# Forget-gate bias and causal mask of the last attention: from GpSimd tiles in SBUF to matmuls in PSUM and VectorE adds

## The reference

```
def odd_layer(x, norm_g, w_in, b_forget, w_out):
    hn = rmsnorm(x, norm_g)
    q, k, v, z, f_logit = jnp.split(hn @ w_in, cuts, axis=-1)      # 16 heads of 128
    log_f = jax.nn.log_sigmoid(f_logit + b_forget)                 # (tokens, 16)
    o = forgetting_attention(q, k, v, log_f)
    return x + (o * jax.nn.silu(z)) @ w_out

# logit[t,s] = q_t.k_s/sqrt(dh) + sum_{s<j<=t} log f_j, causal
    cum = cumsum(log_f)                                            # per head
    s = einsum(q, k) * scale + cq[..., None] - cum[:, :, None, :]
    s = where(kpos <= qpos, s, -inf);  p = softmax(s);  o = einsum(p, v)
```

## Time and profile before

| | |
|---|---|
| median of three executions | 3194.14 us (3189.12 to 3198.18) |
| profiled execution, device time | 3198.18 us |
| its span in the trace | 3196.4 us |
| TensorE busy / VectorE / ScalarE / GpSimd | 94% / 48% / 26% / 9% |
| mean granted TensorE clock | 0.973 of full |

### The profile page before, as it was taken

The page is one execution under the profiler, slowest core; times in us unless marked ns, Lnnn a source line. Parts: engine busy times, 40 slices in busy tenths (PEclk is TensorE's granted clock), DMA queues, the critical chain, the costliest instruction groups (busy, mean ns, idle before and its releaser), DMA issues.

```text
span 3196.4 us, 42548 instructions
## 1 busy us (share of the span) xinstructions
PE 3009.0 (94%) x18244; PEld 2161.4 (68%) x18244; DVE 1547.4 (48%) x1846; ACT 837.8 (26%) x926; POOL 283.5 (9%) x260
## 2 busy tenths in 40 slices
PE   8999999899999999999999999879999998999898
PEld 6777777899977743333333333268858878998886
DVE  4465544674556522222222222357887554444765
ACT  3352221544434310110110110010000243444443
POOL 2042111000000000000000000035440000000100
PEclk9999988999998999999999999989999999999999
DMA  7543221446575599999999999843333355898543
GB/s 244 151 139 100 74 61 58 123 140 182 174 237 171 190 366 425 425 425 425 425 425 425 425 425 425 341 159 118 114 124 118 126 178 125 194 194 183 137 165 138
DMA packets 216144, 725.25 MB, mean 227 GB/s; under 512 B 16314, under 2 KB 18794, under 8 KB 165644
## 3 DMA queue, kind: packets, MB, share of 16 engines
q1 hardware_dynamic: 210716, 702.22, 62.6%
q0 software_dynamic: 4144, 18.14, 1.6%
q10 hardware_dynamic: 1088, 2.10, 0.2%
HBM read 720.28 MB, written 2.11 MB: 226 GB/s over the span
## 4 chain that ended last, share of the span: by engine, by line
PE 72%; DMA 12%; DVE 11%; ACT 4%; issue 1%; POOL 0%; DVEq 0%; ACTq 0%
PE psum L137 71%; DMA t<-in_w_up 12%; DVE t L283 8%; ACT t L254 2%; PE psum L143 2%; DVE t L294 1%; ACT t L256 1%; DVE t L298 1%; DVE t L306 0%; ACT L254 0%; POOL t L328 0%; DVE t L269 0%; ACT L256 0%; DMA t<-in_x 0%; DVE t L275 0%
## 5 line engine op out<-in xcount | busy, mean ns | idle before, releaser
L137 PE MATMUL psum<-t,t 128*128 128x256 f32 (+7 forms) x17166 | 2914.8, 379 | 135.3 <-DVE t L283 78.8
L137 PEld LDWEIGHTS psum<-t,t 128*128 128x128 f32 (+4 forms) x17166 | 2069.7, 175 | 941.2 <-issue 564.2
L283 DVE TENSOR_TENSOR t<-t,t 128x1024 fp32r<-128x1024 f32 (+6 forms) x642 | 786.0, 1224 | 495.8 <-ACT t L254 462.5
L254 ACT ACTIVATE t<-t 128x1024 fp32r<-128x1024 f32 (+8 forms) x521 | 528.6, 1015 | 901.4 <-PE psum L137 625.3
L283 DVE TENSOR_TENSOR t<-t,psum 128x1024 f32<-128x1024 f32 (+3 forms) x265 | 246.3, 929 | 741.3 <-PE psum L137 440.7
L254 ACT ACTIVATE t<-psum 128x1024 f32<-128x1024 f32 (+5 forms) x278 | 213.5, 768 | 1414.9 <-PE psum L137 1315.5
L328 POOL TENSOR_TENSOR t<-t,t 128x1024 f32<-128x1024 f32 (+8 forms) x133 | 222.9, 1676 | 571.7 <-DVE t L283 258.2
L283 DVE TENSOR_TENSOR t<-psum,t 128x1024 f32<-128x1024 f32 (+6 forms) x117 | 101.1, 864 | 121.9 <-PE psum L137 91.8
L143 PE MATMUL psum<-t,t 128*128 128x128 f32 (+1 forms) x566 | 87.9, 294 | 31.7 <-DVE t L294 18.0
L143 PEld LDWEIGHTS psum<-t,t 128*128 128x128 f32 (+1 forms) x566 | 67.6, 150 | 69.5 <-issue 39.8
L83 POOL DMA_DIRECT2D t<-in_s_lr x1 | 0.6, 574 | 1187.2 <-DVE t L306 1187.2
(11 more groups left out here) (67 smaller groups left out, 240.1 us busy)
## 6 DMA issues: line engine op xcount, KB each, us to landing
t<-in_w_gate SPq DMA_DIRECT2D x128, 1024.0 KB, 16.9
t<-in_w_up SPq DMA_DIRECT2D x128, 1024.0 KB, 18.4
t<-in_w_down SPq DMA_DIRECT2D x128, 1024.0 KB, 17.5
t<-in_w_in SPq DMA_DIRECT2D x160, 512.0 KB, 4.1
t<-in_w_in_odd SPq DMA_DIRECT2D x128, 512.0 KB, 5.4
t<-in_w_in_even SPq DMA_DIRECT2D x96, 512.0 KB, 3.8
t<-in_w_out SPq DMA_DIRECT2D x32, 512.0 KB, 4.3
t<-in_w_pg SPq DMA_DIRECT2D x32, 512.0 KB, 4.3
```

Source lines behind the costliest of these rows:

```text
L137: ins = self.e.matmul(o, l, r, start=start, stop=stop, skip_group_check=True)
L254: self.put(self.e.activation(o, i, f, scale=scale), event)
L283: self.put(self.e.tensor_tensor(o, a, b, op), event)
```

## The change

The bias is no longer made as a tile. On TensorE, every score matmul is followed by one more into the same place, which adds F: its stationary operand is a selector `selo` of 16 partitions by 128 columns that holds ones in the row of head h, and its moving operand is F with 16 partitions and 128 or 256 columns. On DVE, each `masked` becomes three operations: an add of the mask on the first 128 columns of both heads, a copy of the middle 128, an add of the mask on the last 128. On GpSimd, the transfers and the eight additions are gone; instead it fills the selector once (a memset and an affine select of 128x2048), after the even layer has released that memory. The wait of `masked` on GpSimd goes; TensorE waits for F and for the selector ahead of scores.

```
-        forget = [alloc(1536).rearrange("p (h x) -> p h x", h=4) for _ in range(2)]
-        f_rows = nc.dram_tensor("f_rows", (16, 256), F32, kind="Internal").ap()
+        selo = alloc(16 * 128).rearrange("p (h t) -> p h t", h=16)
...
-                        pe.wait_ge(("od.q.c", 3), ("od.k.c", 3))
+                        pe.wait_ge(("od.q.c", 3), ("od.k.c", 3), ("od.F",), ("od.sel",))
...
-                            pe.mm(o[:, 0:128], qTo[:, h, 0:128], kTo[:, h, 0:128], True, True)
-                            pe.mm(o[:, 128:384], qTo[:, h, 128:256], kTo[:, h, :], True, True,
+                            pe.mm(o[:, 0:128], qTo[:, h, 0:128], kTo[:, h, 0:128], True, False)
+                            pe.mm(o[:, 0:128], selo[0:16, h, :], F[0][:, 0:128], False, True)
+                            pe.mm(o[:, 128:384], qTo[:, h, 128:256], kTo[:, h, :], True, False)
+                            pe.mm(o[:, 128:384], selo[0:16, h, :], F[0], False, True,
                                   event=("od.s", u, g2) if j else None)
...
-                    v.wait_ge(("od.s", u, g2), ("od.fm", u))
+                    v.wait_ge(("od.s", u, g2))
                     if u > 1:
                         v.wait_ge(("od.p", u - 2, 1))
-                    v.tt(s4[:, 2 * g2:2 * g2 + 2, :], po[:, :, 0:384], forget[u % 2][:, 2 * g2:2 * g2 + 2, :], ALU.add,
-                         event=("od.scored", u) if g2 else None)
+                    v.tt(so[:, :, 0:128], po[:, :, 0:128], cmb, ALU.add)
+                    v.copy(so[:, :, 128:256], po[:, :, 128:256])
+                    v.tt(so[:, :, 256:384], po[:, :, 256:384], cmb, ALU.add)
                     v.free("od.s", u, g2)
...
-            g.wait_ge(("ev.oT", 3), ("ev.oT", 5), ("od.F",))
-            g.load(("landed.rows",), [(f_rows, F[0])])
-            g.wait_ge(("landed.rows",))
-            for u in range(4):
...
-                g.tt(fm[:, :, 0:128], fm[:, :, 0:128], cmb, ALU.add)
-                g.tt(fm[:, :, 256:384], fm[:, :, 256:384], cmb, ALU.add, event=("od.fm", u))
+            g.wait_ge(("ev.oT", 3), ("ev.oT", 5))
+            selector(selo, ("od.sel",))
```

More of the change, by code:

```diff
@@ L2190, in masked @@
                     s4 = scso[u % 2].rearrange("p (h x) -> p h x", h=4)
+                    cmb = cmask.unsqueeze(1).broadcast_to([128, 2, 128])
                     po = v.bank("od.s", u, g2).rearrange("p (a x) -> p a x", a=2)
-                    v.wait_ge(("od.s", u, g2), ("od.fm", u))
+                    so = s4[:, 2 * g2:2 * g2 + 2, :]
+                    v.wait_ge(("od.s", u, g2))
                     if u > 1:
                         v.wait_ge(("od.p", u - 2, 1))
-                    v.tt(s4[:, 2 * g2:2 * g2 + 2, :], po[:, :, 0:384], forget[u % 2][:, 2 * g2:2 * g2 + 2, :], ALU.add,
-                         event=("od.scored", u) if g2 else None)
+                    v.tt(so[:, :, 0:128], po[:, :, 0:128], cmb, ALU.add)
+                    v.copy(so[:, :, 128:256], po[:, :, 128:256])
+                    v.tt(so[:, :, 256:384], po[:, :, 256:384], cmb, ALU.add)
                     v.free("od.s", u, g2)
```

## The result

The changed kernel takes 3217.1 us (median of four executions, 3214.1 to 3222.57) against 3194.2 before: a ratio of 1.0073, 95% interval 1.0054 to 1.009, so 23 us slower (17 to 29). Three more executions of it took 3210.2 to 3220.02 us. The prediction said 3199, between 3191 and 3208. The time lies outside the range, and about five times as far from the kernel before as the forecast.

The account below looks back on a forecast made before the run. TensorE and VectorE were taken to alternate as the bound, with VectorE last in turns 1 to 3. 2.62 + 3 x 0.70 = 4.7 us on the median of 3194.14 gave 3199 us; range 3191 to 3208.

Parts of the forecast that it names:

- So few rows save nothing, and a group gains 1.31 us: Score groups on TensorE: 16-row selector matmuls cost as much as 128-row ones; 2.62 us a turn, 10.5 us in four turns.
- The first rival: Turns 1 to 3: TensorE's price paid in full, 13.3 us if nothing is hidden, 3207.4 us; chance 0.15, including most of it.
- the margin of 0.2 us in turns 2 and 3: Before z13: TensorE would come 0.49 us later, VectorE 0.70 later, so VectorE is last by 0.2 us.
- the wait of 0.98 before z13: Turn 2: third TensorE wait for VectorE in the old timeline, after 0.37 and 1.76; not in the forecast's room.
- the 2.13: Turn 2: TensorE's waits in front of z13, 0.37 + 1.76 us, set against its added 2.62 us.
- half clock behind waits alone: Slow stretches after TensorE waits cost 1.0 to 1.5 us each; taken as zero in the sum, ends +1.5 and -1.5.
- turn 3's slow stretch: After 1.76 us of waiting, granted clock 0.50 over 3050.20 to 3053.60; said to be on the path, -1.5 if it vanishes.
- The sum: Turns 0 to 3: 2.62 us in turn 0 plus 0.70 in each of three turns, together 4.7 us slower.
- the half clock at z7: Turn 1: the wait before z7 grows from 2.78 to 4.6 us; +1.5 if its slow stretch gets longer.
- VectorE's term: Masked adds: three operations for one add cost 0.35 us more a group, 0.70 a turn, on the chain in turns 1 to 3.
- the 2.62 of scores(0): Turn 0: scores(0) stands on TensorE in front of z0, so its whole added 2.62 us is paid.
- GpSimd's side: Selector fill costs nothing, at most +1 us; removed additions return about 1 us of VectorE where TensorE had work: nothing.

Follow-up runs that it names:

- grouped: Changed kernel with each score group's four selector matmuls, still 16 rows, behind the four q.k matmuls of both heads: ratio 1.0017 to the kernel before, +5 us.
- rows64: Changed kernel with selector and F on 64 rows instead of 16: ratio 1.0036 to the kernel before, +12 us.
- rows96: Changed kernel with selector and F on 96 rows instead of 16: ratio 1.0021 to the kernel before, +7 us.
- rows128: Changed kernel with selector and F on 128 rows instead of 16, the added rows zero: ratio 1.0025 to the kernel before, +8 us.
- no_selector: Changed kernel without the 32 selector matmuls, so without the forget bias; VectorE and GpSimd as changed: ratio 1.0005 to the kernel before, +2 us.
- one_add: rows128 with one VectorE add of 128x768 per group, using a constant mask tile, instead of three operations: ratio 1.0003 to the kernel before, +1 us.
- rows16_one_add: Changed kernel's 16-row matmuls with one VectorE add of 128x768 per group, using a constant mask tile: ratio 1.0067 to the kernel before, +21 us.
- grouped_start: Matmul order of grouped, but only the first matmul of a bank has the start flag: ratio 1.0019 to the kernel before, +6 us.

## Why the prediction was wrong

- **The step that failed** is "So few rows save nothing, and a group gains 1.31 us". Its first half holds: grouped shows 16-row matmuls at the price of 128-row ones. The second does not follow. The earlier trace rows are 14 records of 8 rows in a row, and the change sets 16-row matmuls between 128-row ones. A group gained not 1.31 but 2.9 us at full clock (2 x 2.09 - 1.31), eight groups 23.0 and not 10.5, and more at half clock.
- **The trace of before held the price.** In the first block 32-row and 128-row matmuls of 512 columns alternate at full clock. The timeline of the weight loads of before, 250 to 263 us:

```profile
252.49 0.29 PEld L137 LDWEIGHTS psum<-t,t 32*128 32x128 f32 x2 [0.76 <-issue]
253.54 0.30 PEld L137 LDWEIGHTS psum<-t,t 128*128 128x128 f32 x2 [0.76 <-issue]
254.59 0.29 PEld L137 LDWEIGHTS psum<-t,t 32*128 32x128 f32 x2 [0.76 <-issue]
```

  A matmul follows the other by 1.05 us there. Among equal rows its two passes stand 0.43 apart, 0.86 in all, so a change costs 0.2 us, the price measured in the runs. The run of the earlier trace rows shows it too, just outside its window: its passes start 0.11 us apart, and the first one of 128 rows behind it 0.20 after the last.
- **The first rival came true** for a reason that it didn't name. "Every microsecond beyond is paid" held, but the margin of 0.2 us in turns 2 and 3 was too small. In rows64 TensorE has 3.1 us a turn more than the sum gave it, and part 2 grew by 2.69, 2.0 more than the forecast's 0.70: the margin was 1.1. About that comes out if the wait of 0.98 before z13, which the earlier trace rows show, counts as room beside the 2.13; as rows64 still waits 0.92 there, this reason isn't shown. The rival's 13.3 us were too low even so, as they rested on the same 1.31.
- **The clock.** I looked for half clock behind waits alone. It came inside busy groups, and made 10.5 of the 23.75 us (rows64 against changed). The prediction also put turn 3's slow stretch of the kernel before on the path. It cost nothing: part 2 without it takes 33.57 us and part 3 with it 33.58.
- **The sum otherwise held**, as the runs on 96 and 128 rows test it without the failed step: 4.7 forecast, 4.8 in parts 1 to 3 of rows96 and 5.85 in rows128, where the half clock at z7 lasted 6.8 us and not 3.4; +7 (4 to 10) and +8 (5 to 11) by the executions. VectorE's term, 2.1 us forecast, is 2.2 in parts 1 to 3 of rows96 once the 2.62 of scores(0) are taken off, 0.74 a turn in no_selector's parts 2 and 3, and 2.7 in all as rows128 less one_add; where TensorE is last it is 0. GpSimd's side cost and gave nothing, as said.
- **The range** was too narrow: I bounded an alternation of row counts by one row of a uniform run, and gave it no upper end. That a switch of tiling mode drains TensorE is a rule of the Trainium skill (TensorEngine Tiling (Array Packing), Key Properties) which I had not weighed; it speaks against this change.

## What to carry to other kernels

A matmul's price is one of its neighbours too: small operands put between full ones should have as many rows as these (in rows128 and rows96 the rows of zeros cost no time), or stand together in a run. When you price an operation by a run of its own kind, look at the edges of the run and elsewhere in the trace for the mixture that you plan; where there is none, leave the upper end open. And look at weight loads and granted clock, since a TensorE that is 100% busy can run well below its pace, here 2.09 us for a head that takes 1.31 with equal rows, even at full clock.

## What the runs showed of the hardware

- A change between 128-row matmuls and ones of 16, 32 or 64 rows costs 0.2 us at full clock, 0.1 on the pass before it and 0.1 on the pass behind it: the next weight load does not run ahead of its pass, and the row of loads has a gap of 0.33 us behind 256 columns, 0.12 behind 128 and, in the kernel before, 0.76 behind 512. Between 96 and 128 rows there is no such cost. The Trainium skill, TensorEngine Tiling (Array Packing), Key Properties, says that changing the tiling mode, and not just the tile, drains TensorE; by its Available Configurations the row modes are 128, 64 and 32 rows. The traces agree, if 16 rows count as the 32-row mode and 96 as the full array: the gaps of 0.33 us are such drains, and it is this kernel's runs that put the price of 0.2 us on one. That the chip switched its mode is an inference from these gaps; no record names a mode.
- The granted clock fell to 1.2 GHz in score groups without a pause of TensorE: in all four turns with 16 rows in alternation (changed and rows16_one_add), in one with 32, in none with 64 or more, nor with 16 in runs of four. This is one profiled execution a kernel; the mean granted clock of the other executions goes the same way, 0.967 to 0.972 in the changed kernel and 0.974 to 0.976 in rows64. Why it fell stays open.
- In grouped each bank has a second start flag, and the output deviates from the reference by a relative 0.165; with one flag a bank (grouped_start) it does not. That the selector matmul then overwrote the scores in the bank's first 128 columns, instead of adding to them, is inferred. The Trainium skill, PSUM — Partial Sum Buffer, The four PSUM rules, says that a start flag resets the written marks of a whole zone and not only of its own columns; the two runs agree.
